# A hybrid encoder layer on one core: first MLP weight splits moved ahead of the last residual, transposes moved between the first up pieces, and the final norm regrouped

## What is computed

```python
        x = x + rmsnorm(merged @ w_out[l], g_mix_post[l])
        h = rmsnorm(x, g_mlp_pre[l])
        f = jnp.square(jax.nn.relu(h @ w_up[l])) @ w_down[l]
        x = x + rmsnorm(f, g_mlp_post[l])
```

## Time and profile before

| what | us |
|---|---|
| median of three runs | 1625.44 (1623.49 to 1626.95) |
| the profiled execution | 1626.21 |
| its span (first to last record) | 1624.0 |
| around the span | 2.2 |
| PE busy | 1570.5 (97%) |
| DVE busy | 834.5 (51%) |
| ACT busy | 431.1 (27%) |

### The profile page before, as it was taken

How to read it: one execution, slowest core, us unless ns; L and a number is a source line. 1 busy time by engine, 2 the same in 40 slices (tenths; PEclk the granted TensorE clock), 3 DMA queues, 4 the chain that set the end, 5 groups by cost and what they waited for, 6 DMA issues and landing times.

```text
span 1624.0 us, 18388 instructions
## 1 busy us (share of the span) xinstructions
PE 1570.5 (97%) x7423; PEld 1312.5 (81%) x7423; DVE 834.5 (51%) x1590; ACT 431.1 (27%) x588; POOL 120.0 (7%) x193
## 2 busy tenths in 40 slices
PE   6899999999999999999999899999999999999997
PEld 6778769978888888888898788888888888888885
DVE  6849458548458535446766633333333333323348
ACT  5332213233223125221234421213021212111121
POOL 2000000032202212100000200000000000000000
PEclk9999998999999999999999999999999999999998
DMA  8301111141121145414433221111111111111104
GB/s 298 79 26 52 55 68 33 65 130 65 59 97 53 65 117 201 162 51 146 140 117 104 104 91 52 52 42 37 52 52 52 52 52 35 44 50 52 52 1 168
DMA packets 82063, 130.93 MB, mean 81 GB/s; under 512 B 13104, under 2 KB 55120, under 8 KB 82000
## 3 DMA queue, kind: packets, MB, share of 16 engines
q1 hardware_dynamic: 66256, 76.03, 14.4%
q0 software_dynamic: 15744, 54.03, 9.6%
HBM read 104.88 MB, written 25.17 MB: 80 GB/s over the span
## 4 chain that ended last, share of the span: by engine, by line
PE 89%; DVE 6%; DMA 2%; issue 1%; ACT 1%; SPq 0%; POOL 0%; DVEq 0%; ACTq 0%
PE bank L1370 83%; PE bank L1383 1%; PE bank L1587 1%; DMA raw<-in_w_mem_kv_dram 1%; PE bank L1475 1%; PE bank L1601 1%; DVE tok L1340 1%; DVE wlo L297 1%; DVE yst L1332 1%; PE bank L1543 1%; DVE acc L1347 0%; PE bank L1570 0%; DVE stat L839 0%; PE bank L1605 0%; DMA tok<-in_x_dram 0%
## 5 line engine op out<-in xcount | busy, mean ns | idle before, releaser
L1370 PE MATMUL bank<-hThi,whi 128*128 128x512 f32 x1184 | 465.1, 393 | 9.1 <-DVE hTlo L1279 3.8
L1370 PE MATMUL bank<-hTlo,whi 128*128 128x512 f32 x1184 | 463.1, 391 | 0.0
L1370 PE MATMUL bank<-hThi,wlo 128*128 128x512 f32 x1184 | 463.1, 391 | 0.0
L1370 PEld LDWEIGHTS bank<-hThi,whi 128*128 128x128 f32 x1184 | 223.7, 189 | 57.7 <-issue 8.4
L1370 PEld LDWEIGHTS bank<-hThi,wlo 128*128 128x128 f32 x1184 | 223.7, 189 | 47.0
L1370 PEld LDWEIGHTS bank<-hTlo,whi 128*128 128x128 f32 x1184 | 223.9, 189 | 46.2
L291 ACT ACTIVATE whi<-raw 128x2048 fp32r<-128x2048 f32 x65 | 124.3, 1912 | 358.7 <-PE bank L1370 334.9
L1370 PE MATMUL bank<-whi,yhi 128*128 128x512 f32 x512 | 199.3, 389 | 0.8 <-DVE wlo L297 0.8
L1370 PE MATMUL bank<-wlo,yhi 128*128 128x512 f32 x512 | 199.2, 389 | 0.0
L1370 PE MATMUL bank<-whi,ylo 128*128 128x512 f32 x512 | 199.2, 389 | 0.0
L297 DVE TENSOR_TENSOR wlo<-raw,whi 128x2048 fp32r<-128x2048 f32 x65 | 148.9, 2291 | 83.8 <-ACT whi L291 83.6
(11 more groups left out here) (306 smaller groups left out, 1857.5 us busy)
## 6 DMA issues: line engine op xcount, KB each, us to landing
raw<-in_w_in_dram SPq DMA_DIRECT2D x34, 512.0 KB, 4.5
raw<-in_w_up_dram SPq DMA_DIRECT2D x32, 512.0 KB, 4.2
raw<-in_w_down_dram SPq DMA_DIRECT2D x32, 512.0 KB, 4.3
gate_scratch<-scr POOLq DMA_DIRECT2D x48, 256.0 KB, 2.3
tok<-gate_scratch POOLq DMA_DIRECT2D x24, 512.0 KB, 3.6
raw<-in_w_mem_kv_dram SPq DMA_DIRECT2D x8, 512.0 KB, 8.8
y_scratch<-yst POOLq DMA_DIRECT2D x16, 256.0 KB, 2.5
yst<-y_scratch POOLq DMA_DIRECT2D x16, 256.0 KB, 4.2
```

What stands on the lines that cost most here:

```text
L1370: ins = T.matmul(dst, lhs(k)[p], rhs(k)[q], start=start and k == 0 and i == 0, stop=stop and k == kt - 1 and i == 2)
```

## The change

At the entry of the MLP, ACT and DVE split both first up units at tile 7 of stage out, ahead of its residual, instead of the first there and the second at the start of `mlp`. The transposes of tile 6 go ahead of up piece 2 and those of tile 7 ahead of up piece 3, on PE, and ACT and DVE split them there; the event numbers follow. At the exit, each 512-column half of a tile is scaled as soon as it is added, with a factor 32 (the root of 1024) put into the scaling, ACT squares halves into two columns of sums, and DVE finishes tiles 0 to 5 in pairs, with one norm on two columns, and tiles 6 and 7 alone. The last tile's multiply-add and store are done in halves.

```diff
 def out_event(kind, t, e):
     if kind == "h" and t > 5:
-        return FIRST["upA"] + 4 + 2 * (t - 6) + e
+        return FIRST["upA"] + 2 + 3 * (t - 6) + e
...
 def up_event(pc, first):
-    return (FIRST["upA"] if first and pc < 4 else FIRST["mlp"]) + pc
+    return FIRST["upA"] + (0, 1, 4, 7)[pc] if first and pc < 4 else FIRST["mlp"] + pc
...
                         if t == 7 and e == 0:
-                            prep_hi(act, U_MLP, out_event("w", 7, 0))
+                            for u in (U_MLP, U_MLP + 1):
+                                prep_hi(act, u, out_event("w", 7, 0))
...
             def mlp(it, first, last):
-                prep_hi(act, U_MLP + 1, out_event("w", 7, 0) if first else FIRST["mlp"] - 1, it, 4, 24)
+                if not first:
+                    prep_hi(act, U_MLP + 1, FIRST["mlp"] - 1, it, 4, 24)
...
-                    if first and pc == 4:
-                        h2_hi(6)
-                        h2_hi(7)
+                    if first and pc in (2, 3):
+                        h2_hi(pc + 4)
...
-            for t in range(NT):
-                act.wait_ge(acc_done, t + 1)
-                square2("o", acc[:, t, :], 26 + t)
+            n_last = FIRST["mlp"] + 24 * 7 + 8
+            for i, (t, s) in enumerate(LAST_DOWN):
+                wait_taken(act, n_last + i)
+                if i < 2:
+                    act.wait_ge(sq_o, NT)
+                    act.wait_ge(sq_x, NT)
+                else:
+                    act.wait_ge(sq_f, i - 1)
+                column = (26 if s == 0 else 10) + t
+                A.activation(scr[:, i % 2, :], acc[:, t, s * 512:s * 512 + 512], ACT.Square,
+                             accum_out=sumsq[:, column:column + 1]).then_inc(sq_f, 1)
...
                     if t == 7:
                         prep_lo(dve, U_MLP)
+                        prep_lo(dve, U_MLP + 1)
                     residual(t)
...
-            def scale(t):
-
-                mark(V.tensor_tensor(yx[:, t % 2, :], acc[:, t, :], tok[:, 0:D], mul))
-
-            def finish(t):
-
-                xt = tok[:, (1 + t % 3) * D:(2 + t % 3) * D]
-                dve.wait_ge(sq_o, NT + t + 1)
-                rstd(sumsq[:, 26 + t:27 + t])
-                dve.wait_ge(x1_back[t % 3], 16 * (t // 3 + 1))
-                V.scalar_tensor_tensor(out=xt, in0=yx[:, t % 2, :], scalar=stat[:, 1:2], in1=xt, op0=mul, op1=add).then_inc(out_made, 1)
+            def finish(tiles):
+
+                c, n = slice(tiles[0], tiles[-1] + 1), len(tiles)
+                v, nv, y, w = (stat[:, 2 * k:2 * k + n] for k in (0, 1, 2, 3)) if n == 1 else \
+                    (stat[:, 0:2], stat[:, 2:4], rs[:, 0:2], stat[:, 4:6])
+                dve.wait_ge(sq_f, LAST_DOWN.index((tiles[-1], 1)) + 1)
+                do(V.scalar_tensor_tensor(out=v, in0=sumsq[:, 26:34][:, c], scalar=D * EPS, in1=sumsq[:, 10:18][:, c], op0=add, op1=add))
+                mark(V.tensor_scalar(nv, v, -0.5, None, mul))
+                do(V.tensor_scalar(y.bitcast(i32), v.bitcast(i32), -0.5, RSQRT_SEED, mul, add))
+                for _ in range(3):
+                    if n == 1:
+                        do(V.scalar_tensor_tensor(out=w, in0=y, scalar=nv, in1=y, op0=mul, op1=mul))
+                    else:
+                        do(V.tensor_tensor(w, y, y, mul))
+                        do(V.tensor_tensor(w, w, nv, mul))
+                    do(V.scalar_tensor_tensor(out=y, in0=w, scalar=1.5, in1=y, op0=add, op1=mul))
+                for k, t in enumerate(tiles):
+                    xt = tok[:, (1 + t % 3) * D:(2 + t % 3) * D]
+                    dve.wait_ge(x1_back[t % 3], 16 * (t // 3 + 1))
+                    for h in ([slice(0, D)] if t < NT - 1 else [slice(0, 512), slice(512, D)]):
+                        V.scalar_tensor_tensor(out=xt[:, h], in0=yx[:, t % 2, h], scalar=y[:, k:k + 1], in1=xt[:, h], op0=mul, op1=add)\
+                            .then_inc(out_made, 1)
...
-                if s == 0 and t >= 2:
-                    finish(t - 1)
-                if s == 1:
-                    wait_taken(dve, n)
-                    wait_taken(dve, n_last + LAST_DOWN.index((t, 0)))
-                    dve.sem_inc(acc_done, 1)
-                    scale(t)
-                    if t == 1:
-                        finish(0)
-            finish(NT - 1)
+                wait_taken(dve, n)
+                mark(V.scalar_tensor_tensor(out=yx[:, t % 2, h], in0=acc[:, t, h], scalar=float(D) ** 0.5, in1=tok[:, h],
+                                            op0=mul, op1=mul))
+                if s == 1 and t in (1, 3, 5):
+                    finish((t - 1, t))
+                elif s == 1 and t > 5:
+                    finish((t,))
```

More of the change, by code:

```diff
@@ L255, in hybrid_layer @@
         f_sq, f_hi, f_lo = sem("f_sq"), sem("f_hi"), sem("f_lo")
-        acc_done = sem("acc_done")
+        sq_f = sem("sq_f")
         last_gain = sem("last_gain")
@@ L363, in _ @@
                 sp.wait_ge(out_made, t + 1)
-                sp.dma_start(out[0, t * P:(t + 1) * P, :], tok[:, (1 + t % 3) * D:(2 + t % 3) * D]).then_inc(out_sent[t % 3], 16)
-            for s, count in enumerate((3, 3, 2)):
+                if t < NT - 1:
+                    sp.dma_start(out[0, t * P:(t + 1) * P, :], tok[:, (1 + t % 3) * D:(2 + t % 3) * D]).then_inc(out_sent[t % 3], 16)
+            c = (1 + (NT - 1) % 3) * D
+            sp.dma_start(out[0, (NT - 1) * P:, 0:512], tok[:, c:c + 512]).then_inc(out_sent[1], 16)
+            sp.wait_ge(out_made, NT + 1)
+            sp.dma_start(out[0, (NT - 1) * P:, 512:D], tok[:, c + 512:c + D]).then_inc(out_sent[1], 16)
+            for s, count in enumerate((3, 4, 2)):
                 sp.wait_ge(out_sent[s], 16 * count)
@@ L1298, in mlp @@
             def mlp(it, first, last):
-                prep_lo(dve, U_MLP + 1, it, 4)
+                if not first:
+                    prep_lo(dve, U_MLP + 1, it, 4)
                 for pc, (s, c, hf) in enumerate(UP_FIRST if first else UP_LATER):
                     n, ct, h = up_event(pc, first), 2 * s + c, slice(hf * 512, hf * 512 + 512)
-                    if first and pc == 4:
-                        h2_lo(6)
-                        h2_lo(7)
+                    if first and pc in (2, 3):
+                        h2_lo(pc + 4)
                     if pc == (6 if first else 4):
@@ L1690, in mlp @@
                     u, n, c = U_MLP + s, up_event(pc, first), slice(cc * P, cc * P + P)
+                    if first and pc in (2, 3):
+                        h2_transposes(pc + 4)
                     if first and pc == 4:
-                        h2_transposes(6)
-                        h2_transposes(7)
                         for t in range(4, NT):
```

## The result

The changed kernel takes **1612.82 us** (median of four runs, 1610.27 to 1614.34) against 1625.14 for the kernel before: a ratio of 0.9926, 95% interval 0.9913 to 0.9939. The forecast was 1612.6 within 1610.4 to 1616.4. The profiled execution took 1614.34 us, its span is 1612.6.

The account below looks back on a forecast made before the run. PE, busy 1570.5 of 1624.0 us, was taken as the bound, with DVE bounding the exit. Entry 10.1 plus exit 2.7 gave 12.8 us off 1626.21, so 1613.4, or 1612.6 us against the median, range 1610.4 to 1616.4.

Parts of the forecast that it names:

- fixed points of the entry: PE at MLP entry, from piece 1's end (913.34) to piece 4's start, forecast at 925.98 instead of 936.09: 10.1 us gained.
- both holes: PE's waits ahead of up pieces 2 and 4, about 2.8 and 3.9 us, forecast to close with no new one.
- The clock's share: Lower granted clock on PE's matmuls behind the entry's two waits, about 1.7 us each, counted in the 10.1 us gain.
- The slacks: Time producers have to spare at the entry: 2.7 us for h2 of tile 6, 2.3 us at piece 4.
- The residual's delay: DVE at the entry: tile 7's residual starts 1.0 us later, behind the second unit's early low-part split.
- Exit: Behind PE's last matmul: 2.07 us less on DVE and 0.6 in the store, together 2.7, bounds 1.5 and 3.0.
- The store's part: Last tile's store in halves at the exit: 0.6 us less, bounds -0.3 to 0.6.
- Rival D: PE ahead of piece 2: h2 of tile 6 over 2.7 us late, slower than before, about 1628 at 16 late; chance 0.03.
- A: At the entry the clock falls behind each of two transpose groups, 3.4 us less gain, 1616.0 us; chance 0.07.
- B: Splits of tile 7 late at piece 4, 2.7 us less gain, 1615.3 us; chance 0.07.
- C: Exit gives nothing because reloads or stores take back DVE's gain, 1615.3 us; chance 0.04.
- E: Holes only move, to piece 3 or the down events; time within noise, 1624 us; chance 0.03.

Follow-up runs that it names:

- entry_only: Kernel before with only the change's entry lines (event numbers, early split, moved transposes) and the old exit: 1615.21 us, ratio 0.9939.
- before_again_1: Kernel before, unchanged, profiled again: 708.21 us from tile 5's transposes to PE's last matmul, against 709.92 in the first profile.
- dve_late_1: Changed kernel with the second up unit's low part computed twice on DVE: 699.85 us from tile 5's transposes to PE's last matmul, no wait.
- dve_late_2: Changed kernel with the second up unit's low part computed three times on DVE: 702.13 us from tile 5's transposes to PE's last matmul.
- transposes_x4: Changed kernel with each transpose of tiles 6 and 7 done four times: 705.08 us from tile 5's transposes to PE's last matmul.

## Why the prediction was right, step by step

- **The fixed points of the entry.** Forecast for piece 4, counted from piece 1's end: 12.64 us. Measured: 927.18 - 914.52 = 12.66. The gain of 10.1 came out as 10.08 against the same profile. With it, the mechanism forecast (both holes closed, no new one, the clock up) is what the traces show.
- **The clock's share of it** was mis-sized as a property of the program. I put in 3.4 us from one trace; four traces give 1.7 to 4.0, 3.0 in the mean. Against a median the entry's term is better written as 6.7 of waits plus 3.0, or 9.7. The medians of `entry_only` give 1624.79 - 1615.21 = 9.6, but their interval would hold 10.1 as well. That the profile's 3.4 lay so near the mean is luck: from `before_again_1` the same sum would have had 1.7 us less.
- **The slacks.** 2.7 forecast at tile 6's transposes; 914.52 - 911.77 = 2.75 measured, and `dve_late_1` and `dve_late_2` bracket it and place it at 2.7. 2.3 forecast at piece 4; 927.18 - 924.96 = 2.2 measured. The residual's delay was put at 1.0; it starts 1.65 us behind ACT's copy (904.60 - 902.95) where it started 0.70 behind it before, so 0.95.
- **Exit.** Last add at 1614.26 forecast, which is 2.38 us behind PE's end at 1611.88, and 1605.36 - 1602.98 = 2.38 measured; norm 1.47 behind it, measured 1.47; norm 1.78, measured 1.79. End of the last multiply-add 6.93 us behind PE's end forecast, 7.05 measured: the two halves take 1.41 together, not 0.61 + 0.69. Scaling a half, for which no row stood, took 0.69 with 0.61 held, as taken. So DVE's part is 1.95 instead of 2.07: its last row ended 9.00 behind PE before, 7.05 now. The store's part is 0.55 instead of 0.6 (3.12 behind DVE's end before, 2.57 now). Together 2.5 instead of 2.7.
- **The sum against the medians.** With the clock's mean and the exit as measured the gain is 9.7 + 2.5 = 12.2 us; the medians give 1625.14 - 1612.82 = 12.3, where the forecast had 12.8. It still came within 0.2 us of the median, since the median of the kernel before, taken with one run more, fell by 0.3 to 1625.14. So the last tenths of the agreement are luck: single runs of the changed kernel differ by 4 us.
- **Slips in the working.** The range takes 11.4 as the least gain, but its own bounds give 10.1 + 1.5 = 11.6. Rival D gives tile 6's transposes 15 us of slack before; rows of the first profile give 928.75 - 909.67 = 19, and 15 to 16 is tile 7's. Neither moves the forecast.
- **Rivals.** A (clock behind the transposes) is out by the new entry's starts in every trace, and by `transposes_x4` at four times the length. B is out, with 2.2 us to spare. C is out: the reloads were in time and the tail is 2.5 shorter. D has its mechanism and its threshold confirmed by `dve_late_2`, at a delay that the kernel doesn't have; what D named as its cause, a late load of old x, was in no run. E is out by the stretch.

## What to carry to other kernels

A step that one engine waits for should be costed by the consumer's new schedule between two points that don't move, with the slack of every producer worked out beside it; the removed waits then need not be summed one by one, and two edits that fill the same hole aren't counted twice (2.6 and 4.7 us of waits alone, 6.7 together). When the engine behind the bound has a little less time per tile than it needs, as DVE had at the exit with 5.59 against 5.45 us, a lag is never worked off; there, sharing the norm's small instructions between two tiles brought 1.6 of the exit's 2.5 us. A clock's fall read from one profile is one draw: look at several traces before it goes into a sum. Compare traces over the stretch that the change touches, since the rest of the program may vary by more than the effect.

## What the runs showed that I had not expected

The granted clock behind one and the same hole differs between executions of the same kernel: behind 2.61 idle us it stayed up in two traces and fell in two, and behind 3.75 to 3.78 us it cost between nothing and 2.8 us. Behind 1.74 and 1.83 idle us it stayed up in the one trace each. Thirty-two transposes in a row, 3.4 us, did not bring it down. And the front of the program, ahead of tile 5's transposes, varied by 5.3 us over fourteen traces with no difference in PE's work there. Where that comes from is open.
